# A two-layer transformer block on one core: the head of each layer reordered, squares of x moved behind the first products

## The reference

```python
for l in range(DEPTH):                                   # DEPTH = 2
    xn = rms_norm(x, attn_norm[l])                       # x * rsqrt(mean(x*x) + EPS) * g
    (nsa_q, kv_c, kv_s, kv_w, nsa_g, cq, ckv, k_rope_raw,
     gate_a, gate_b) = split_cols(xn @ w_in[l])
    o_a = nsa_attention(nsa_q, kv_c, kv_s, kv_w, nsa_g, cmp_pe[l], cmp_w1[l], cmp_w2[l], pos)
    o_b = mla_attention(cq, ckv, k_rope_raw, mla_q_norm[l], mla_kv_norm[l], mla_w_uq[l], mla_w_ukv[l], pos)
    merged = (jax.nn.sigmoid(gate_a) * (o_a @ nsa_w_o[l]) + jax.nn.sigmoid(gate_b) * (o_b @ mla_w_o[l]))
    x = x + merged @ w_out[l]
    hn = rms_norm(x, mlp_norm[l])
    x = x + jnp.square(jax.nn.relu(hn @ w_up[l])) @ w_down[l]
return rms_norm(x, final_norm)
```

## Time and profile before

| | us |
|---|---|
| median of 3 runs | 1550.94 (1549.37 to 1550.97) |
| the profiled execution | 1549.4 |
| its span | 1547.5 |
| mean granted TensorE clock | 0.997 of full speed |
| PE busy | 1508.3 |
| DVE busy | 890.0 |
| ACT busy | 723.9 |

### The profile page before, as it was taken

The page is one execution under the profiler, slowest core; times in us unless marked ns, Lnnn a source line. Parts: engine busy times, 40 slices in busy tenths (PEclk is TensorE's granted clock), DMA queues, the critical chain, the costliest instruction groups (busy, mean ns, idle before and its releaser), DMA issues.

```text
span 1547.5 us, 23290 instructions
## 1 busy us (share of the span) xinstructions
PE 1508.3 (97%) x7404; PEld 1260.6 (81%) x7404; DVE 890.0 (58%) x1537; ACT 723.9 (47%) x1316; POOL 437.4 (28%) x456
## 2 busy tenths in 40 slices
PE   6999999999999999999999999999999999999997
PEld 5888888888888888888888788787878888888886
DVE  6765755766654444535556757566675535354455
ACT  6753777874432222222366547777744212222233
POOL 1301666775010100101021036767730201010011
PEclk9999999999999999999999999999999999999999
DMA  5333212125222222322324422111352222223223
GB/s 194 109 130 123 91 67 76 42 89 173 100 95 96 95 95 95 96 95 99 105 69 136 150 82 83 56 69 57 96 176 96 96 95 96 101 94 104 95 95 109
DMA packets 43273, 155.56 MB, mean 101 GB/s; under 512 B 5312, under 2 KB 5312, under 8 KB 43168
## 3 DMA queue, kind: packets, MB, share of 16 engines
q1 hardware_dynamic: 36864, 133.19, 25.6%
q0 software_dynamic: 5728, 19.00, 3.6%
q10 hardware_dynamic: 576, 2.10, 0.4%
HBM read 143.78 MB, written 10.49 MB: 100 GB/s over the span
## 4 chain that ended last, share of the span: by engine, by line
PE 80%; issue 9%; DVE 3%; POOL 3%; ACT 2%; DMA 1%; POOLq 0%; DVEq 0%; ACTq 0%
PE G L1375 13%; PE G L1377 13%; PE G L1376 13%; PE O L1377 8%; PE O L1376 8%; PE O L1375 8%; PE O L1648 3%; PE T L1624 3%; PE S L1599 2%; PE T L1375 1%; PE T L1376 1%; PE T L1377 1%; POOL wsplit L492 1%; PE O L1450 1%; DVE F L1326 1%
## 5 line engine op out<-in xcount | busy, mean ns | idle before, releaser
L599 ACT ACTIVATE wsplit<-stage 128x1024 fp32r<-128x1024 f32 x229 | 242.4, 1058 | 608.9 <-PE G L1377 280.4
L927 DVE TENSOR_TENSOR wsplit<-stage,wsplit 128x1024 fp32r<-128x1024 f32 x181 | 264.3, 1460 | 70.7 <-ACT wsplit L599 64.1
L1375 PE MATMUL G<-xg,wsplit 128*128 128x512 f32 x592 | 238.6, 403 | 12.4 <-DVE xg L931 10.8
L585 POOL TENSOR_TENSOR F<-Y 128x512 f32<-128x512 f32 x64 | 68.4, 1069 | 637.3 <-DVE Y L1343 637.3
L1377 PE MATMUL G<-xg,wsplit 128*128 128x512 f32 x592 | 231.6, 391 | 0.0
L1376 PE MATMUL G<-xg,wsplit 128*128 128x512 f32 x592 | 231.6, 391 | 0.0
L492 POOL TENSOR_TENSOR wsplit<-stage,wsplit 128x1024 fp32r<-128x1024 f32 x48 | 116.1, 2419 | 138.3 <-ACT wsplit L599 137.8
L1134 DVE CUSTOM_DVE_ANT_0 F<-S,F 128x512 f32<-128x512 f32 x192 | 93.7, 488 | 101.6 <-PE S L1599 64.4
L1375 PEld LDWEIGHTS G<-xg,wsplit 128*128 128x128 f32 x592 | 111.6, 189 | 37.2 <-DVE xg L931 13.8
L754 ACT ACTIVATE F<-F,nmx 128x512 f32<-128x512 f32 x192 | 107.7, 561 | 64.9 <-DVE nmx L1134 63.1
L1377 PEld LDWEIGHTS G<-xg,wsplit 128*128 128x128 f32 x592 | 111.4, 188 | 24.4
(11 more groups left out here) (286 smaller groups left out, 3001.9 us busy)
## 6 DMA issues: line engine op xcount, KB each, us to landing
stage<-units SPq DMA_DIRECT2D x230, 512.0 KB, 3.3
stage_n<-units_n SPq DMA_DIRECT2D x22, 512.0 KB, 3.3
gates<-Y POOLq DMA_DIRECT2D x32, 256.0 KB, 2.7
E<-gates POOLq DMA_DIRECT2D x24, 256.0 KB, 3.7
x<-x_in ACTq DMA_DIRECT2D x4, 512.0 KB, 7.1
F<-gates POOLq DMA_DIRECT2D x8, 256.0 KB, 3.8
rope<-tables POOLq DMA_DIRECT2D x1, 768.0 KB, 7.1
out<-F SPq DMA_DIRECT2D x3, 256.0 KB, 2.2
```

The source lines that it names most:

```text
L585: pool.tensor_tensor(F[:, m % 2, :], Y[:, m % 2, :], Y[:, m % 2, :], ALU.mult)\
L599: act.activation(wslot(u)[:, 0, :], staged(u), ACT.Copy).then_inc(s_whin if u in SN else s_whi, 1)
L927: dve.tensor_tensor(wslot(u)[:, 1, :], staged(u), wslot(u)[:, 0, :], ALU.subtract)\
L1375: pe.matmul(dst, a(0), b(0), start=first, stop=False)
```

## The change

The first rows. SP now issues the parameters, the first unit in two halves, three double rows of x and the second unit, and ACT only the first two rows of x, one by one. POOL asks for the constants and rope tables once rows 4 and 5 of x have landed, where it waited for rows 2 and 3. PE multiplies ones by ones 18 times (`WARM`) before anything else. Rows of x are split without squaring them, and the first unit's halves are split between the first rows.

The layer's head. In both layers the squares of all rows are taken by ACT after it has rounded VC, and summed by DVE after it has written VC's rest. The squares that the end of the first layer takes of the same rows are still taken; only the last row's sum is left out there. `mean_square` follows VC on PE instead of KC, and `spread` stands in KS before its fifth square instead of in VC before its sixth. V0 is rounded on ACT ahead of `spread` and `swap(0)`, where it followed `swap(0)`.

The end. PE sums the last squares from two tiles, `F[:, 2]` and `F[:, 1]`, with twice the matmuls, and DVE no longer adds the last row.

The diff, without unchanged lines around it:

```diff
@@ -158,0 +159,2 @@
+SQ, SQADD = 3 * KT, 3 * KT - 1
+
@@ -182,0 +185,2 @@
+WARM = 18
+
@@ -364 +368,2 @@
-        s_x = sems("s_x0", "s_x1", "s_x2", "s_x3")
+        s_x = sems("s_x0", "s_x1", "s_x23", "s_x45", "s_x67")
+        s_wfirst, s_hifirst, s_lofirst = sems("s_wfirst", "s_hifirst", "s_lofirst")
@@ -429,5 +434,7 @@
-            for slot in range(2):
-                if slot == 1:
-                    sp.wait_ge(s_x[2], 16)
-                sp.dma_start(stage[:, slot, :], units[slot]).then_inc(s_w[slot], 16)
-            sp.wait_ge(s_x[3], 16)
+            sp.dma_start(par_all[:, :], params).then_inc(s_params, 16)
+            sp.dma_start(stage[:, 0, 0:512], units[0][:, 0:512]).then_inc(s_wfirst, 16)
+            sp.dma_start(stage[:, 0, 512:1024], units[0][:, 512:1024]).then_inc(s_w[0], 16)
+            for i in range(1, 4):
+                sp.dma_start(x[:, 2 * i:2 * i + 2, :], x_in[:, 2 * i:2 * i + 2, :]).then_inc(s_x[i + 1], 16)
+            sp.dma_start(stage[:, 1, :], units[1]).then_inc(s_w[1], 16)
+            sp.wait_ge(s_x[4], 16)
@@ -464 +470,0 @@
-            pool.dma_start(par_all[:, :], params).then_inc(s_params, 16)
@@ -467 +473 @@
-            pool.wait_ge(s_x[1], 16)
+            pool.wait_ge(s_x[3], 16)
@@ -601,2 +607 @@
-            def square(n, m, x_ready, gain):
-                act.wait_ge(s_gfree, x_ready)
+            def row_square(l, n, m):
@@ -604 +609 @@
-                    act.wait_ge(s_sqadd, n * KT + (m - 1))
+                    act.wait_ge(s_sqadd, l * SQADD + (n * KT + m - 1))
@@ -605,0 +611,2 @@
+
+            def row_hi(m, gain):
@@ -607,0 +615,5 @@
+            def square(l, n, m, x_ready, gain):
+                act.wait_ge(s_gfree, x_ready)
+                row_square(l, n, m)
+                row_hi(m, gain)
+
@@ -616,2 +628,2 @@
-            for i in range(4):
-                act.dma_start(x[:, 2 * i:2 * i + 2, :], x_in[:, 2 * i:2 * i + 2, :]).then_inc(s_x[i], 16)
+            for i in range(2):
+                act.dma_start(x[:, i, :], x_in[:, i, :]).then_inc(s_x[i], 16)
@@ -620 +631,0 @@
-            split_hi(0, 0)
@@ -623,2 +634,8 @@
-                act.wait_ge(s_x[m // 2], 16)
-                square(0, m, GFREE0 - KT + (m + 1), par_all[:, PR_ATTN + m:PR_ATTN + m + 1])
+                act.wait_ge(s_x[m if m < 2 else m // 2 + 1], 16)
+                row_hi(m, par_all[:, PR_ATTN + m:PR_ATTN + m + 1])
+                if m == 0:
+                    act.wait_ge(s_wfirst, 16)
+                    act.activation(wslot(0)[:, 0, 0:512], staged(0)[:, 0:512], ACT.Copy).then_inc(s_hifirst, 1)
+                if m == 1:
+                    act.wait_ge(s_w[0], 16)
+                    act.activation(wslot(0)[:, 0, 512:1024], staged(0)[:, 512:1024], ACT.Copy).then_inc(s_whi, 1)
@@ -795,0 +813,3 @@
+                for m in range(KT):
+                    row_square(l, 0, m)
+                split_hi(l, BIG[2])
@@ -801 +821 @@
-                    if u in BN and item != ("GATE", FIRST_GATE - 1):
+                    if 0 < u and u in BN and item != ("GATE", FIRST_GATE - 1):
@@ -803,2 +822,0 @@
-                    if u == 0:
-                        spread(l * 2)
@@ -805,0 +824,2 @@
+                        spread(l * 2)
+                        swap(0)
@@ -832 +852 @@
-                    if item in ROPED:
+                    if item in ROPED and u > 0:
@@ -894 +914 @@
-                    square(l * 2 + 1, m, l * NG + (G_OUT + m + 1 + GFREE0), par[:, PR_MLP + m:PR_MLP + m + 1])
+                    square(l, 1, m, l * NG + (G_OUT + m + 1 + GFREE0), par[:, PR_MLP + m:PR_MLP + m + 1])
@@ -914 +934,3 @@
-                    square(l * 2 + 2, m, (l + 1) * NG + (GFREE0 - KT + m + 1), nextgain[:, m:m + 1])
+                    square(l, 2, m, (l + 1) * NG + (GFREE0 - KT + m + 1), nextgain[:, m:m + 1])
+                act.wait_ge(s_sqadd, l * SQADD + SQADD)
+                act.wait_ge(s_sq, l * SQ + SQ)
@@ -933,2 +955,2 @@
-            def norm_sum(n, m, gain):
-                dve.wait_ge(s_sq, n * KT + (m + 1))
+            def row_sum(l, n, m):
+                dve.wait_ge(s_sq, l * SQ + (n * KT + m + 1))
@@ -937 +959 @@
-                        dve.wait_ge(s_sqadd, n * KT + m)
+                        dve.wait_ge(s_sqadd, l * SQADD + (n * KT + m))
@@ -938,0 +961,2 @@
+
+            def row_lo(n, m, gain):
@@ -941,0 +966,8 @@
+
+            def first_lo(u):
+                return dve.tensor_tensor(wslot(u)[:, 1, 0:512], staged(u)[:, 0:512], wslot(u)[:, 0, 0:512], ALU.subtract)
+
+            def second_lo(u):
+                return dve.tensor_tensor(wslot(u)[:, 1, 512:1024], staged(u)[:, 512:1024], wslot(u)[:, 0, 512:1024],
+                                         ALU.subtract)
+
@@ -953 +984,0 @@
-            split_lo(0, 0)
@@ -955 +986,7 @@
-                norm_sum(0, m, par_all[:, PR_ATTN + m:PR_ATTN + m + 1])
+                row_lo(0, m, par_all[:, PR_ATTN + m:PR_ATTN + m + 1])
+                if m == 0:
+                    dve.wait_ge(s_hifirst, 1)
+                    first_lo(0).then_inc(s_lofirst, 1)
+                if m == 1:
+                    split_rounded(dve, 0, 0)
+                    second_lo(0).then_inc(s_wlo[0], 1)
@@ -1198,0 +1236,2 @@
+                for m in range(KT):
+                    row_sum(l, 0, m)
@@ -1203,0 +1243 @@
+                split_lo(l, BIG[2])
@@ -1209 +1248,0 @@
-                        split_lo(l, BIG[2])
@@ -1333 +1372,2 @@
-                    norm_sum(l * 2 + 1, m, par[:, PR_MLP + m:PR_MLP + m + 1])
+                    row_sum(l, 1, m)
+                    row_lo(l * 2 + 1, m, par[:, PR_MLP + m:PR_MLP + m + 1])
@@ -1363,2 +1403,8 @@
-                    down(QUARTERS - 1, k, k < KT - 1)
-                    norm_sum(l * 2 + 2, k, nextgain[:, k:k + 1])
+                    down(QUARTERS - 1, k, k < KT - 2)
+                    if k == KT - 2:
+                        split_rounded(dve, l, NU)
+                        first_lo(NU).then_inc(s_lofirst, 1)
+                        second_lo(NU).then_inc(s_wlo[BN[NU] % 2], 1)
+                    if k < KT - 1:
+                        row_sum(l, 2, k)
+                    row_lo(l * 2 + 2, k, nextgain[:, k:k + 1])
@@ -1392,2 +1438,2 @@
-            def mean_square(n):
-                pe.wait_ge(s_sqadd, n * KT + KT)
+            def mean_square(l, n):
+                pe.wait_ge(s_sqadd, l * SQADD + (n * KT + KT))
@@ -1402,0 +1449,3 @@
+            pe.wait_ge(s_init, 1)
+            for tt in range(WARM):
+                pe.matmul(SB[0][:, 0:P], ones[:, :], ones[:, :], start=True, stop=True)
@@ -1560,0 +1610,5 @@
+                def rows_in(k):
+                    if k == 4:
+                        unit(UNIT["KC", 0])
+                    pe.wait_ge(s_xlo, l * 16 + (k + 1))
+
@@ -1575 +1629,5 @@
-                        project(item, lambda k: pe.wait_ge(s_xlo, l * 16 + (k + 1)))
+                        pe.wait_ge(s_lofirst, l + 1)
+                        free(item)
+                        tile(g_tile(item)[:, :], UNIT[item], xg, rows_in)
+                    elif name == "VC":
+                        project(item)
@@ -1578,3 +1636,3 @@
-                        mean_square(l * 2)
-                    elif name == "VC":
-                        project(item, lambda k: spread(l * 2) if k == 5 else None)
+                        mean_square(l, 0)
+                    elif name == "KS":
+                        project(item, lambda k: spread(l * 2) if k == 4 else None)
@@ -1752 +1810 @@
-                            mean_square(l * 2 + 1)
+                            mean_square(l, 1)
@@ -1775,0 +1834,6 @@
+            def last_squares(src, first):
+                for tt in range(QT):
+                    ins = pe.matmul(SB[1][:, tt:tt + 1], src[:, tt * P:(tt + 1) * P], ones[:, 0:1],
+                                    start=first and tt == 0, stop=not first, skip_group_check=True)
+                return ins
+
@@ -1781 +1845,4 @@
-            mean_square(L * 2)
+            pe.wait_ge(s_sqadd, L * SQADD)
+            last_squares(F[:, 2, :], True)
+            pe.wait_ge(s_sq, L * SQ)
+            last_squares(F[:, 1, :], False).then_inc(s_ms, 1)
```

More of the change, by code:

```diff
@@ L599, in split_hi @@
                 act.activation(wslot(u)[:, 0, :], staged(u), ACT.Copy).then_inc(s_whin if u in SN else s_whi, 1)
-            def square(n, m, x_ready, gain):
+            def row_square(l, n, m):
+                if m >= 3:
+                    act.wait_ge(s_sqadd, l * SQADD + (n * KT + m - 1))
+                act.activation(F[:, m % 2 if m > 0 else 2, :], x[:, m, :], ACT.Square).then_inc(s_sq, 1)
+            def row_hi(m, gain):
+                act.activation(xg[:, 0, m, :], x[:, m, :], ACT.Copy, scale=gain).then_inc(s_xhi, 1)
+            def square(l, n, m, x_ready, gain):
                 act.wait_ge(s_gfree, x_ready)
-                if m >= 3:
-                    act.wait_ge(s_sqadd, n * KT + (m - 1))
```

(10 more changed lines are left out.)

## The result

The changed kernel takes 1564.5 us (median of 6 runs, 1563.1 to 1569.1), the kernel before 1549.6 in the same measurements (1549.2 to 1551.0): ratio 1.0094, 95% interval 1.0083 to 1.0106. That is 15 us slower, where 10 were forecast: the direction and its cause came out as forecast, and the time lies at the very top of the range given (1564.5).

The account below looks back on a forecast made before the run. The prediction took the ACT and DVE chain from spread to Q0 as the bound, so later spreads cost time: 5.9 (layer 1) + 3.4 (layer 0) + 0.7 (end) = 10.0 us, giving 1561 us, range 1554.5 to 1564.5.

Parts of the forecast that it names:

- The bound: Both layers: a chain of ACT and DVE from the spread, not PE's work, sets Q0's start, 27.7 us behind the spread.
- Layer 1: Head of layer 1: VC's matmuls, sums and mean square put the spread 5.9 us later; bounds 5.7 and 6.9.
- Layer 0: Head of layer 0: waiting for constants and later spread outweigh the faster start, 3.4 us later; bounds -0.2 and +4.3.
- The constants' landing: Start of layer 0: the moment DVE's cast ahead of VC's rest can go on, taken as 16.0; bounds 12.4 and 16.9.
- the table's issue: Start: POOL issues the rope table's load behind rows 4 and 5 of x, at 9.0 to 9.8 against 9.31 before.
- the clock rival: Pauses ahead of VC and KW drop PE to half rate, six matmuls costing 1.4 us: 1562 to 1565; chance 0.13.
- the 2 to 2.5 forecast: Both layers: a new PE wait of 2 to 2.5 us ahead of Q0, besides 4 to 5 ahead of KW.
- V0: Both layers: rounding V0 ahead removes its 1.49 us wait, but waits at KW and Q0 replace it; worth 0.
- The end: End of kernel: DVE's last sum leaves the path, PE's sums of squares double; +0.7 us, bounds -0.7 and +0.8.
- late constants: Part of the range's top, layer 0: constants land at 16.9 instead of 16.0.
- dear sums: Part of the range's top, layer 1: a sum on DVE costs 0.85 us, spread 6.9 us later instead of 5.9.
- part of the clock: Part of the range's top: some of the half-rate cost behind new PE pauses, which in full gave 1562 to 1565.

Follow-up runs that it names:

- experiment 1: Kernel before with only mean square moved behind VC, spread into KS, and V0 and KS rounded ahead; 1560.7 us, ratio 1.0069.
- experiment 7: Changed kernel with the end as before: DVE adds the last row, PE sums squares from one tile; 1565.1 us in a single execution.
- experiment 4: Changed kernel with DVE's cast waiting only for the masks, on their own semaphore, not the rope tables; 1558.8 us, ratio 1.0058 to the kernel before.
- experiment 5: Kernel before with only ACT's swap(0) moved behind V0's rounding; 1551.8 us, ratio 1.0011.
- experiment 3: Changed kernel with 50 products of ones instead of 18; 1562.9 us, ratio 1.0081 to the kernel before.

## Why the prediction was right, and what in it was off

**The bound.** "Q0's start is the spread's start plus 27.7 us" held: 28.04 and 28.01 in the changed kernel, 27.7 with the spread moved forward, 27.9 and 27.6 with it moved back. Moving the spread to the front by 1.5 us in layer 0 and 1.2 in layer 1 (from KC's start) made the kernel 2.7 us faster at the same mean clock; moving it 5.4 and 5.8 us to the back made the profiled span 11.2 us longer.

**Layer 1.** Forecast 5.9 us from the spread; measured 6.0 at the spread and 6.3 at Q0. Each piece stands in the rows: VC's rest at its old distance behind the layer's first matmul within 0.3 us, seven sums in 5.13 us (forecast 5.04), the spread 3.67 behind the mean square's start. The forecast had the sums on DVE as the bound of KS by 0.25 us; the trace has PE, with 0.05 us to spare, and experiment 1 confirms it. That hardly changes the size, but it changes what the time was lost to: PE's own matmuls, not the sums.

**Layer 0.** Forecast 3.4 with bounds of -0.2 and +4.3, measured 7.5 at the spread, 7.8 at Q0 and 8.5 at the layer's end: outside its own bounds. The mechanism was right (the cast waits for the constants, and all stands behind it), two sizes were off. The constants' landing was taken as 16.0 and bounded by 16.9; it was 17.68. The term that failed is the table's issue, "at 9.0 to 9.8 against 9.31": POOL's wait for rows 4 and 5 ended at 9.3, so the issue was at 10.56, and the transfer was no shorter (7.1 us) though fewer holes were left. That is 1.7 us.

The other 2.5 us are the clock rival, which I gave 0.13 and priced at 1.1 for this place: I let it last six matmuls, as at the start, and it lasted through twelve of VC's 24, two thirds of its time. (In experiment 7, with the same head and a pause of 5.86 us, VC took 7.25 us, so there it cost 1.7.) Behind 5.64 us of idleness the granted clock was 0.52 from 18 to 25 us; with 1.65 us of it, in experiment 4, the same 24 matmuls ran at 1.00. The Trainium skill, in "TensorE: Matmul & The Clock Gate", section "What's actually happening", has half rate as the state into which an idle TensorE falls back, and out of which activity brings it. The trace agrees. Ahead of KW the same fall costs little, since Q0 waits for the chain anyway (0.75 and 0.36 us of idle time are left of the 2 to 2.5 forecast). The forecast and this rival were not exclusive, as I had them: the first makes the pause, the second follows. Experiment 4 has both pieces right at once: its spread follows the cast by 10.99 us, where the sum has 11.1.

**V0.** Forecast worthless, and it is: alone it makes the kernel 0.1% slower (1.0011).

**The end.** Forecast +0.7, measured +0.8, by the cause named.

**The sum.** 10.0 us were forecast, 15.0 measured in the medians and 15.5 in the two profiled spans. Of the 5.5 us between, the two sizes in layer 0 make 4.1 at the spread (7.45 against 3.4), the stretch of low clock behind Q0 is 0.7, and the slightly longer way from spread to Q0 0.3 in each layer. That the time still lies within the range is luck. The top of the range, 1564.5, is 13.6 us above the 1550.9 that I started from, and the measured difference is 15.0; but the kernel before came out at 1549.6 in the final measurements, not at 1550.9. The top was also put together from other parts: late constants (they came later than its 16.9), dear sums (they were not dear) and part of the clock.

## What to carry to other kernels

Where PE is 97% busy and still waits now and then, look for the chain on the other engines that sets its next wait, and measure its length from the event that starts it: if two occurrences agree to 0.02 us and both end in idle time, it is that chain, and only the moment of its start matters. Work that is put on the engine that issues the first link, ahead of that link, costs its full length each time: here PE's matmuls of VC and KS ahead of the spread. What runs on another engine beside that work costs nothing as long as it ends in time: the seven sums on DVE just did, and in experiment 7, where they took 0.3 us longer, KS waited 0.21 us. When a start gets faster, see which load the next instruction of each list names in its wait: the one that nobody felt before is the next bound, and a pause of PE there can cost a second time, through the clock.

## What the runs showed of the hardware that was not expected

- A pause of TensorE of 5.64 us was followed by 5.3 us at half the rate (0.43 against 0.23 us from one matmul of 512 columns to the next), longer than the six matmuls of the kernel's start; the pauses of 4.83 and 4.80 us ahead of KW were followed by 3 to 4 us of it (45.48 to 48.6 and 812.62 to 816.6); behind the pauses of 1.65 and 1.64 us ahead of VC none is seen. In between it goes either way: in experiment 5 the granted clock was 0.51 from 52.9 to 56.3, shortly behind a pause of 2.12 us ahead of Q0 in layer 0, and 1.00 from 814 to 820, around the one of 2.15 us in layer 1.
- The granted clock also fell for 3.4 us in a stretch without a pause, right behind 24 products of a single column (from 96.5 and 864.5 in the changed kernel, from about 848.5 in the one before); in layer 0 of the one before, behind the same products, it didn't. Of the nine traces, five have such a stretch in layer 0 and seven in layer 1; it begins between the last of these products and 1.5 us behind them, and lasts 3.4 us, once 6.8.
- A 768 KB load on POOL's queue took 6.8 to 7.3 us from issue to landing in eight traces and 9.3 in the ninth, experiment 3, which has the same other loads as the changed kernel (7.1).
